# The last, three-expert stage of a decoder trunk: gathers moved ahead, a third buffer for low weights, row sums and transposes in another order

## The reference

```python
def moe_swiglu(h, w_router, b_router, w_gate, w_up, w_down):
    logits = (t @ w_router + b_router)
    top_vals, top_idx = lax.top_k(logits, 2)
    gates = sum(one_hot(top_idx, 8) * softmax(top_vals)[..., None], axis=1)   # 256 x 8
    for e in range(8):
        out = out + gates[:, e:e + 1] * ((silu(t @ w_gate[e]) * (t @ w_up[e])) @ w_down[e])
```

## Time and profile before

| | |
|---|---|
| runs (median; lowest, highest) | 1613.69 us; 1611.99, 1618.89 |
| profiled execution, its span | 1611.64 us, 1608.9 us |
| PE busy, DVE busy, ACT busy (share of the span) | 94%, 80%, 64% |
| last narrow product ends, first half of the trio starts | 1183.2, 1193.6 us from the start |
| second half of the trio starts, last one ends | 1204.3, 1590.0 us |
| HBM read | 461.15 MB, 287 GB/s over the span |

### The profile page before, as it was taken

The page is one execution under the profiler, slowest core; times in us unless marked ns, Lnnn a source line. Parts: engine busy times, 40 slices in busy tenths (PEclk is TensorE's granted clock), DMA queues, the critical chain, the costliest instruction groups (busy, mean ns, idle before and its releaser), DMA issues.

```text
span 1608.9 us, 23502 instructions
## 1 busy us (share of the span) xinstructions
PE 1514.5 (94%) x8591; PEld 1260.1 (78%) x8591; DVE 1286.9 (80%) x1426; ACT 1023.9 (64%) x1045; POOL 217.3 (14%) x251
## 2 busy tenths in 40 slices
PE   6997999998889699999999999999989999999996
PEld 4776899998659678888888888888877777777774
DVE  4796566556875598898899889889868988899886
ACT  4556555455123487687777687777748777778773
POOL 0771146521770000000000000000000000000000
PEclk9998999999789899999999999999999999999998
DMA  9954386656484689999999999999818999999991
GB/s 307 331 195 168 106 284 231 236 193 236 158 262 148 220 315 367 361 340 370 363 341 357 374 350 355 365 351 354 306 53 314 340 338 344 340 313 338 376 379 40
DMA packets 231208, 463.30 MB, mean 288 GB/s; under 512 B 18255, under 2 KB 57687, under 8 KB 231127
## 3 DMA queue, kind: packets, MB, share of 16 engines
q1 hardware_dynamic: 229591, 461.55, 80.6%
q10 hardware_dynamic: 1536, 0.68, 0.2%
HBM read 461.15 MB, written 1.05 MB: 287 GB/s over the span
## 4 chain that ended last, share of the span: by engine, by line
PE 75%; DVE 11%; ACT 4%; POOL 4%; issue 3%; DMA 1%; SPq 1%; DVEq 0%; ACTq 0%; POOLq 0%
PE bank L2163 12%; PE bank L2166 12%; PE bank L2169 12%; PE bank L1823 12%; DVE wlo L1744 4%; PE bank L1978 3%; PE bank L2305 3%; PE bank L2302 3%; PE bank L2257 2%; PE bank L2258 2%; PE bank L2265 2%; PE bank L2270 2%; PE bank L2269 2%; DVE bank L1315 2%; PE bank L1907 2%
## 5 line engine op out<-in xcount | busy, mean ns | idle before, releaser
L1597 DVE TENSOR_TENSOR wlo<-ring,whi 128x2048 fp32r<-128x2048 f32 x210 | 477.0, 2289 | 68.5 <-PE bank L2169 55.6
L1020 ACT ACTIVATE whi<-ring 128x2048 fp32r<-128x2048 f32 x210 | 400.9, 1918 | 117.7 <-PE bank L2166 117.7
L1744 DVE TENSOR_TENSOR wlo<-ring,whi 128x2048 fp32r<-128x2048 f32 x126 | 283.1, 2281 | 26.2 <-PE bank L2270 25.0
L1117 ACT ACTIVATE whi<-ring 128x2048 fp32r<-128x2048 f32 x126 | 238.4, 1912 | 37.7 <-PE bank L2265 22.9
L2163 PE MATMUL bank<-whi,xe_hi 128*128 128x512 f32 x560 | 219.7, 392 | 7.2 <-ACT whi L1020 7.2
L2166 PE MATMUL bank<-whi,xe_lo 128*128 128x512 f32 x560 | 218.9, 391 | 0.0
L1233 DVE TENSOR_TENSOR ring_lo<-ring,ehi 128x2048 fp32r<-128x2048 f32 x45 | 106.3, 2362 | 58.3 <-ACT ehi L786 58.2
L2169 PE MATMUL bank<-wlo,xe_hi 128*128 128x512 f32 x560 | 150.5, 391 | 0.0
L2163 PEld LDWEIGHTS bank<-whi,xe_hi 128*128 128x128 f32 x560 | 105.8, 189 | 29.4 <-issue 7.3
L2169 PEld LDWEIGHTS bank<-wlo,xe_hi 128*128 128x128 f32 x560 | 105.7, 189 | 22.1
L2166 PEld LDWEIGHTS bank<-whi,xe_lo 128*128 128x128 f32 x560 | 105.8, 189 | 21.9
(11 more groups left out here) (450 smaller groups left out, 2829.4 us busy)
## 6 DMA issues: line engine op xcount, KB each, us to landing
ring<-in_moe_w_gate_dram SPq DMA_DIRECT2D x112, 1024.0 KB, 7.1
ring<-in_moe_w_up_dram SPq DMA_DIRECT2D x112, 1024.0 KB, 6.8
ring<-in_moe_w_down_dram SPq DMA_DIRECT2D x112, 1024.0 KB, 6.7
ring<-in_mod_w_dram SPq DMA_DIRECT2D x24, 2048.0 KB, 9.8
ring<-in_ffn_w_gate_dram SPq DMA_DIRECT2D x11, 1024.0 KB, 6.1
ring<-in_ffn_w_up_dram SPq DMA_DIRECT2D x11, 1024.0 KB, 8.7
ring<-in_ffn_w_down_dram SPq DMA_DIRECT2D x11, 1024.0 KB, 5.2
ring<-in_conv_w_pw_dram SPq DMA_DIRECT2D x8, 1024.0 KB, 12.3
```

The costliest lines, as they stand in the source:

```text
L1020: act.activation(whi[:, n % HI_SLOTS, :], ring[:, s * HW:(s + 1) * HW], ACT.Copy).then_inc(hi_ready, 1)
L1117: act.activation(whi[:, q % HI_SLOTS, :], ring[:, s * HW:(s + 1) * HW], ACT.Copy).then_inc(hi_ready, 1)
L1597: v.tensor_tensor(wlo[:, n % LO_SLOTS, :], ring[:, s * HW:(s + 1) * HW], whi[:, n % HI_SLOTS, :].bitcast(F32), ALU.subtract).then_inc(lo_r ...
L1744: v.tensor_tensor(wlo[:, q % LO_SLOTS, :], ring[:, s * HW:(s + 1) * HW], whi[:, q % HI_SLOTS, :].bitcast(F32), ALU.subtract).then_inc(lo_r ...
```

## The change

It touches only the end of the narrow loop and the trio. Arithmetic and results stay the same.

1. `last_high`, `last_low`, `last_combined`, `last_combine`: what stood between the narrow loop and the trio is put into functions that the trio calls later. ScalarE makes the high parts of halves 0 to 2 first, then `last_high`, then copies `xb` and `xs`. VectorE makes the low part of half 0, then `last_low`, the low part of half 1, `xb`, `xs`, the low part of half 2, and `last_combined`. TensorE gathers `xb` and `xs`, transposes the small selection (to bank GA), does half 0, transposes the wide selection (to bank GB), and then does the last combine.
2. `wlo_third`: low weights have three slots (two old ones and one more in sbuf), and the wait for a slot is for the half three earlier. The ring keeps six slots; other buffers are moved to make room.
3. `T_OFFSET` is 3 for the transposes of the wide expert, but for its last block.
4. On VectorE, at half q: `sums` of a G ahead of the low part of q; `sums` of a U and the rest of `hidden_rows` behind it. On ScalarE the copies that `sums` waits for go ahead of the other one.

```diff
-T_OFFSET = {x: 1 if (x[0], x[2]) == SMALL_G[-1] else 2 for x in G_ENDS}
+T_OFFSET = {x: 1 if (x[0], x[2]) == SMALL_G[-1] else 3 if x[0] == 0 and x[2] < FT - 1 else 2 for x in G_ENDS}
+TRIO_LO = 3
...
+        wlo_third = at("wlo_third", [P, HW], 76 * KB, F32R)
...
+        def trio_lo(q):
+            return wlo_third[:, :] if q % TRIO_LO == 2 else wlo[:, q % TRIO_LO, :]
...
 # ScalarE
                     if j:
                         act.wait_ge(he_ready, i * FT + j)
                         act.wait_ge(sum_hid, GI[(0, j - 1)])
+                    act.activation(uBt[:, :], psum[UB][TAIL:P, :], ACT.Copy).then_inc(low_rows, 1)
                     act.activation(uA[:, :], psum[UA][:, :], ACT.Copy).then_inc(wide_u, 1)
-                    act.activation(uBt[:, :], psum[UB][TAIL:P, :], ACT.Copy).then_inc(low_rows, 1)
...
                 elif o == 0:
-                    act.activation(silu_g[:, :], psum[GA][:, :], ACT.Silu).then_inc(s_ready, 1)
                     if j:
                         act.wait_ge(trio_t, GI[(0, j - 1)])
                     act.activation(gBt[:, :], psum[GB][TAIL:P, :], ACT.Copy).then_inc(low_rows, 1)
+                    act.activation(silu_g[:, :], psum[GA][:, :], ACT.Silu).then_inc(s_ready, 1)
...
             def trio_item(i):
+                for q in range(3):
+                    trio_high(q, i)
+                last_high(i)
                 act.wait_ge(tail_gath, 1)
                 act.activation(xb[:, :, 0:TAIL], ...).then_inc(tail_xh, 1)
+                for g in range(2):
+                    act.wait_ge(tail_gath, g + 2)
+                    act.activation(xs[:, :, 4 * g:4 * g + 4, 0:TAIL], ...).then_inc(tail_xh, 1)
+                act.wait_ge(sel_t, i + 1)
+                act.activation(selTS[:, :], psum[GA][:, :], ACT.Copy).then_inc(trio_selT, 1)
+                for q in range(3, NQ):
+                    trio_high(q, i)
+                    if q == 3:
+                        act.wait_ge(sel_t, i + 2)
+                        act.activation(selTW[:, :], psum[GB][:, :], ACT.Copy).then_inc(trio_selT, 1)
...
 # VectorE
+            def trio_low(q, i):
+                s = q % TRIO_SLOTS
+                v.wait_ge(hi_ready, i * NH + (q + 1))
+                v.wait_ge(lo_used, i * NH + (q + 1 if q < 2 else q))
+                v.tensor_tensor(trio_lo(q), ring[...], whi[...], ALU.subtract).then_inc(lo_ready, 1)
...
+                trio_low(0, i)
+                last_low(i)
+                trio_low(1, i)
                 v.wait_ge(tail_xh, 1)
                 v.tensor_tensor(xb[:, :, TAIL:P], ...).then_inc(tail_xl, 1)
+                for g in range(2):
+                    v.wait_ge(tail_xh, g + 2)
+                    v.tensor_tensor(xs[:, :, 4 * g:4 * g + 4, TAIL:P], ...).then_inc(tail_xl, 1)
+                trio_low(2, i)
+                last_combined(i)
+                for q in range(3, NQ):
+                    ended = AFTER.get(q - 3, (0, "D"))[1]
+                    if ended == "G":
                         sums(q - 3, i)
-                    if AFTER.get(q - 3, (0, "D"))[1] == "G":
-                        hidden_rows(q - 3, i)        # had sums(q, i) in it
                     if q - 3 in T_AT:
                         dve_low(T_AT[q - 3], i)
...                                                    # small_out, small_low, scattered as before
+                    trio_low(q, i)
+                    if ended == "U":
+                        sums(q - 3, i)
+                    if ended == "G":
+                        hidden_rows(q - 3, i)
...
 # TensorE
                 ins.then_inc(tail_gath, 1)           # xb gathered
+                pe.wait_ge(tail_sel, 8)
+                pe.wait_ge(yx_ready, i * 2 + 2)
+                small_gather(0)
+                small_gather(1)
+                pe.wait_ge(hl_ready, i * FT)
+                (four transposes of selS to psum[GA]).then_inc(sel_t, 1)
                 for q, (o, kind, j, h) in enumerate(TRIO):
                     ...
                     if q == 0:
-                        pe.wait_ge(acc_half, NCOMB)
-                        pe.wait_ge(tail_sel, 8)
-                        small_gather(0)
-                        small_gather(1)
-                        (four transposes of selS to psum[SG])
                         (four transposes of sel, selB to psum[GB]).then_inc(sel_t, 1)
+                        pe.wait_ge(tail_xl, 3)
+                        last_combine(i)
```

More of the change, by code:

```diff
@@ L1044, in _, with last_high @@
                                        ACT.Copy).then_inc(xh_ready, 1)
-            y_high(narrow, 0)
-            act.wait_ge(yx_ready, narrow * 2 + 2)
-            act.activation(yx_hi2[:, :], y_exp[:, 512:1024], ACT.Copy).then_inc(yxh_ready, 1)
+            def last_high(i):
+                y_high(i, 0)
+                act.wait_ge(yx_ready, i * 2 + 2)
+                act.activation(yx_hi2[:, :], y_exp[:, 512:1024], ACT.Copy).then_inc(yxh_ready, 1)
             def ended(q, i):
@@ L1138, in _ @@
                 trio_item(narrow)
+            with act.Else():
+                last_high(narrow)
             act.activation(fin_scrap[:, :], ones[:, 0:2], ACT.Abs_reciprocal_sqrt)
@@ L1638, in _, with last_low, last_combined @@
                                     None, ALU.is_equal).then_inc(tail_sel, 1)
-            evac_y(narrow)
-            y_low(narrow, 0)
-            y_low(narrow, 1, yx_hi2)
-            for m in range(NCOMB):
-                combined(narrow, m, psum[WIDE_EXTRA[m]], acc_half)
+            def last_low(i):
+                evac_y(i)
+                y_low(i, 0)
+                y_low(i, 1, yx_hi2)
+            def last_combined(i):
+                for m in range(NCOMB):
+                    combined(i, m, psum[WIDE_EXTRA[m]], acc_half)
             def sums(q, i):
@@ L1662, in hidden_rows @@
                     v.tensor_tensor(hid_e[:, :], silu_g[:, :], uA[:, :], ALU.mult).then_inc(he_ready, 1)
-                sums(q, i)
                 m = SMALL_G.index((o, j)) if o else 0
@@ L1771, in _ @@
                 trio_item(narrow)
+            with v.Else():
+                last_low(narrow)
+                last_combined(narrow)
             v.wait_ge(act_own, 2 * TILES + 2 * TB)
@@ L2210, in _, with last_combine @@
                         ins.then_inc(t_done, 1)
-            pe.wait_ge(selT_ready, narrow)
-            for m in range(NCOMB):
-                combine(narrow, m, psum[WIDE_EXTRA[m]], (yx_hi, yx_hi2)[m // 2])
+            def last_combine(i):
+                pe.wait_ge(selT_ready, i)
+                for m in range(NCOMB):
+                    combine(i, m, psum[WIDE_EXTRA[m]], (yx_hi, yx_hi2)[m // 2])
             def small_gather(g):
@@ L2243, in wide_steps @@
                     else:
-                        pe.wait_ge(tail_xl, 1)
+                        pe.wait_ge(trio_selT, 2)
                 a_, b_ = (UA, UB) if kind == "U" else (GA, GB)
@@ L2337, in trio_item @@
                 ins.then_inc(tail_gath, 1)
+                pe.wait_ge(tail_sel, 8)
[3 more added lines that the diff above has]
+                pe.wait_ge(hl_ready, i * FT)
+                for e in range(2):
+                    for tb in range(TB):
+                        ins = nc.tensor.transpose(psum[GA][:, (e * TB + tb) * P:(e * TB + tb + 1) * P], selS[:, e, tb, :], ident[:, :])
+                ins.then_inc(sel_t, 1)
                 for q, (o, kind, j, h) in enumerate(TRIO):
@@ L2379, in _ @@
                 trio_item(narrow)
+            with pe.Else():
+                last_combine(narrow)
 _INS = ["x", "c", "mod_w", "mod_b", "norm1_g", "norm2_g", "conv_w_pw1", "conv_b_pw1", "conv_w_dw",
```

80 lines of the change are left out of this document (32 added, 48 removed).

## The result

The changed kernel takes 1585.97 us, median of four runs (1582.53 to 1590.37); the kernel before took 1612.84 beside it (four runs). The ratio is 0.983 [0.981, 0.985]: 27 us less, and the interval lies clear of the 0.5% (8 us) within which the prediction calls a result no difference. The profiled execution took 1582.53 us with a span of 1580.7, before 1611.64 and 1608.9.

What follows compares the result with a forecast made beforehand. PE was taken to set the end, idling for low weights and hidden values from DVE. 14.3 + 8.4 + 6.2 = 28.9, less 1 for loads and 1 for ACT's copies, gave 27 us: 1587 us, range 1579 to 1602.

Steps and rivals of the forecast that it cites:

- 2 us off for loads and for ACT's copies: Deduction from the summed gain: 1 us for loads, 1 us where ACT's copy keeps DVE waiting without a lead.
- 1198 to 1563: Sign in the trace: the trio's second half starts near 1198 and its last half ends near 1563.
- Third low slot: Trio loop: low weights ready 2 to 4 us early, plain stalls go; gain 18.8 - 4.5 = 14.3 us.
- the stalls that I meant to keep: Trio loop: PE stalls expected to remain, such as where four small halves follow each other; 4.5 us in all.
- Later wide transposes: Trio loop: with offset 3 the 1.4 us wait at wide transposes goes six times, 8.4 us; last block keeps its wait.
- the floor: Trio loop: PE's own work sums to 356.2 of 385.7 us, so at most 29.5 us can be won there.
- Row sums ahead, the product behind: DVE in the trio: a low part covers 16.2 us of silu waits, keeping 96% load possible; gain not counted separately.
- cover of 1.2 us for the small transposes: Trio's small blocks: product ready about 5.1 us behind its G, transposes 6.3 behind, so the later multiply costs nothing.
- Start: Start of the stage: PE's waits of 2.17 and 2.48 us and half 0's slow clock go; gain 6.2 us.
- Loads: Trio: weight loads just keep up with the faster PE; 1 us taken where small halves lie close.
- DVE as the bound: Rival, trio loop: new waits on ACT's copies make DVE the bound, about 13 us stay away: 1600 us; chance 0.14.
- slower: Rival, trio: low parts over 1.2 us late make small transposes wait 2.2 us each, 14 times: 1630 us; chance 0.05.

Runs made afterwards that it cites:

- a1: Kernel before with the new start alone (two slots, old VectorE order, offset 2; ScalarE's copies in new order): 1601.70 us, ratio 0.992.
- n2: Kernel before with third slot and new start (old VectorE order, offset 2; ScalarE's copies in new order): 1583.22 us, ratio 0.982.
- a4: Kernel before with offset 3 alone (two slots, old start, old VectorE order; ScalarE's copies in new order): 1607.82 us, ratio 0.997.
- u3: The change with row sums and products ahead of the low part again on VectorE (ScalarE's copies stay new): 1584.47 us, ratio 0.982.
- u2: The change with the wide transposes two halves behind their G again (offset 2): 1594.29 us, ratio 0.988 to the kernel before.
- u1: The change with the low weights in two slots again: 1616.99 us, ratio 1.001 to the kernel before.
- a3: Kernel before with VectorE's new order alone (two slots, offset 2, old start; ScalarE's copies in new order): 1651.82 us, ratio 1.023.
- n1: The change with products ahead of the low part in two blocks and the first scatter's two adds behind them: 1580.20 us, ratio 0.980 to before.
- u4: The change with the start of the stage as in the kernel before: 1590.81 us, ratio 0.986 to the kernel before.
- a2: Kernel before with the third slot alone (old start, old VectorE order, offset 2; ScalarE's copies in new order): 1589.25 us, ratio 0.986.

## Why the prediction was right, and where it was not

**The time and the sum** (1587, a gain of 27; measured 1586, a gain of 27). The loop's two terms together, 14.3 + 8.4 = 22.7, were what the loop gave, 22.7. The split between them was wrong. And the forecast took 2 us off for loads and for ACT's copies, which puts the loop at 365 (1198 to 1563 among its signs); it took 363.0, so nothing of these 2 us showed. The trace of the change gives 22.7 + 6.6 - 1.1 = 28.2 us of span. That the medians agree within 1 us is luck: the change's four runs lie between 1582.5 and 1590.4, and its repeat gave a gain of 31.

**Third low slot, 14.3: mis-sized.** With the small swap in both kernels the slot takes the loop from 381.4 (a1) to 363.8 (n2), 17.6 us. Of these 10.5 are waits for low weights, less than the 14.3 that I put on them, and 5.2 are waits at the wide transposes. What I missed is that DVE, once ahead, also has the hidden values ready earlier; that was part of the next term. Of the stalls that I meant to keep, 4.5 and the last wide block's 1.4, the change shows 4.4 in places above 0.2 us: 2.06 where the first expert is scattered (forecast 2.0 to 2.4), 1.33 at the last wide block, about 0.6 near the end and 0.46 early on.

**Later wide transposes, 8.4: the step that failed.** "The wait of 1.4 goes six times" held on the kernel before, where the wide transposes' loss fell from 10.5 to 0.9 (a4), though half of it by the small swap: it and offset 3 bring 4.3 each. Beside the slot in the old order it brings 0.4 (n2 363.8, u3 363.4): the wait it removes is no longer there. Both terms counted idle time that had one cause, DVE's lateness, and I sized them by separate groups of the waits. That their sum is right is owed in part to the floor, since together they could not take more than the 29.5 us lost less what I kept, and in part to luck: the slot brought 3.3 more than its term, the small swap, which had no term, brought 4.3, and offset 3 brought 8.0 less.

**Row sums ahead, the product behind: wrong in its reason.** I wrote that this gain "is what keeps DVE's 96% possible". u3 has 10.7 us of silu waits back and the same time. A wait on an engine that is ahead costs lead first; only 4.5 us of it reached PE as waits for low weights, and the transposes gave 4.1 back. The new order brings 0.4 with offset 3 (u3, the change), costs 9.4 with offset 2 (n2, u2), and 19 to 42 with two slots (a4 to u1, a1 to a3). So offset 3, which I priced as a gain, mostly pays for what the order costs. The order has a use all the same: with the products ahead of the low part in its two worst blocks, and the scatter's adds behind them, the loop is 360.7 (n1), 2.7 below the old order's. My cover of 1.2 us for the small transposes was too large: in the change the product ends 1.23 us ahead of the transposes at two of the fourteen blocks, 0.4 to 0.75 ahead at nine, and at three they start as soon as it ends (0.06). PE waited over 0.2 us at two of them, without the lead at thirteen.

**Start, 6.2: right.** 6.6 in the change, 6.65 by u4, and the same by a1. (The three items that I named add up to 6.35; 6.2 is what the new timeline gave.) Half 0 ran at the full granted clock, and the old start shows again the wait (2.5) with slow matmuls behind it (0.478 us each on average, 0.40 in the change).

**Loads, 1 us: none needed.** In the change ACT's list holds no wait for a load; the most that a loop here shows is 0.5 us, once (n2), and 0.4 in two places (u3). The loop moves 340 GB/s (I said 345); late in it the change moved 383, and u3 399 over the 75 us from 1465 to 1540. The Trainium skill, "SBUF — State Buffer", summary of rules for kernel authors, has about 358 GB/s for HBM to SBUF; these rows stand above it, so for this kernel on one core the measurement decides. The skill's "Perfetto Trace Analysis", section on engine utilization, says that a core whose pair is idle can draw more than its share of 358, up to about 435; with that these rows agree.

**The rivals.** DVE as the bound would have shown as PE waiting all along with DVE busy; DVE was busy 340 of 364 us with PE 359. The "slower" one had the right mechanism and a wrong condition: I let it begin with a low part that starts 1.2 us late for ACT's sake. It begins with a DVE that waits for a slot, and it then costs PE 1.3 on average at a small transpose, not 2.2, but up to 3.2 at a wide one (a3). u1 and a3 are that case.

**Not foreseen:** the small swap's 4.3 us with two slots (what it is worth beside the third no run shows, since no kernel has the slot without it), and the tail, 1.1 us longer in the profiled execution, by the granted clock alone. The tail is no effect of the change: it took 17.5 us in u3 and 20.4 in a4.

## What to carry to other kernels

Before adding up idle terms, ask which of them have one cause: a buffer that lets the producer run ahead removed most of the waits that this producer's lateness showed, wherever they stood (24.7 us of them became 7.9), and a fix aimed at one group was then worth 0.4 us instead of 4.3. Moving work behind a long instruction is safe only while the engine is ahead and its reader has time: the same reordering was neutral with three slots and the later transposes, cost 9 us with three slots and the early ones, and 42 us of loop with two. When such a reordering comes out neutral, see whether it moved a loss: putting the products first in its two worst blocks, and two adds later, won 2.3 us. So test parts of a change in pairs, since neither "undo one" nor "do one alone" shows a cost that another part pays back.

## What the runs showed of the hardware

In u3 the loads kept 399 GB/s over 75 us at a DMA share of 1.03, with a median of 9.4 us from issue to landing of a 1 MB load. At the same place the change had 383 GB/s and 8.2 us, and the kernel before 388 GB/s (over 40 us) and 7.6. Latency grew with the rate, and six ring slots covered it: ACT waited 0.4 us for loads in u3.

Around the last wait of PE (3.3 us) the granted clock does not do the same in each run: it fell to 1.2 GHz between 2.1 and 4.7 us behind the last product in most profiles and came back while PE's last matmuls ran; in u3 and a2 it fell only when PE had finished. The tails of all profiled executions lie between 17.5 and 20.4 us for identical work. What sets the moment no run here tells. A difference of 2 us between two single profiles of this kernel is therefore to be sought first in its tail.
